# Second boundary turned from the residual itself, its root applied in the V, U and Z panels; first attention with four banks for head 0's logits

## The reference

```python
# first block
logits = q @ k * 64**-0.5 + bias         # banded attention, 16 heads, 128-token blocks, window +-128
x = x + rmsnorm(mixed, post_mix)
h = rmsnorm(x, pre_mlp)
f = square(relu(h @ w_mlp_in)) @ w_mlp_out
x = x + rmsnorm(f, post_mlp)             # residual 2
# second block, layer A
u, v, z = split(rms_norm(x, a_pre) @ a_w_in, 3)     # 3 x 2048 columns
v = layer_norm(gelu(v))
y = gelu(u) * (w_s v + b_s) * silu(z)
# rms_norm(x, g) = x * rsqrt(mean(x*x) + eps) * g, the root is one number per token
```

## Time and profile before

| | |
|---|---|
| median of 3 runs | 1885.99 us (1885.85 to 1886.63) |
| the profiled execution | 1886.83 us, its span 1885.0 us |
| PE busy (matmul) | 1819.4 us (97%) |
| PE weight load busy | 1511.0 us (80%) |
| DVE, ACT, POOL busy | 900.7, 855.2, 843.0 us (48%, 45%, 45%) |
| mean granted TensorE clock | 0.986 |
| chain that ended last | PE 80%, DVE 8%, issue 6%, ACT 3%, POOL 1% |

### The profile page before, as it was taken

How to read it: one execution, slowest core, us unless ns; L and a number is a source line. 1 busy time by engine, 2 the same in 40 slices (tenths; PEclk the granted TensorE clock), 3 DMA queues, 4 the chain that set the end, 5 groups by cost and what they waited for, 6 DMA issues and landing times.

```text
span 1885.0 us, 27143 instructions
## 1 busy us (share of the span) xinstructions
PE 1819.4 (97%) x9064; PEld 1511.0 (80%) x9064; DVE 900.7 (48%) x1331; ACT 855.2 (45%) x1795; POOL 843.0 (45%) x601
## 2 busy tenths in 40 slices
PE   8999999999899999999999999989999999999998
PEld 7787887888787788887988888867888888887776
DVE  4787898888414565234331033050063311446754
ACT  4655545555334656334442244243533332456662
POOL 4644555556453121444444444444364444432322
PEclk9999999999899999999999999989999999999999
DMA  5822121111133131332233333324232223221111
GB/s 173 145 79 68 56 67 56 59 64 57 45 101 118 35 106 39 97 131 91 89 90 101 99 92 100 99 71 155 78 109 81 90 85 100 84 70 57 58 44 56
DMA packets 46223, 159.85 MB, mean 85 GB/s; under 512 B 4763, under 2 KB 7195, under 8 KB 45884
## 3 DMA queue, kind: packets, MB, share of 16 engines
q1 hardware_dynamic: 38592, 140.53, 24.0%
q10 hardware_dynamic: 7548, 18.20, 3.9%
HBM read 152.42 MB, written 6.29 MB: 84 GB/s over the span
## 4 chain that ended last, share of the span: by engine, by line
PE 80%; DVE 8%; issue 6%; ACT 3%; POOL 1%; DVEq 0%; ACTq 0%; POOLq 0%
PE main L300 61%; PE main L328 4%; PE aux L772 3%; PE main L1702 2%; PE aux L759 1%; DVE u_acc L1904 1%; PE aux L746 1%; PE aux L372 1%; PE aux L603 1%; DVE x_res L547 1%; PE aux L627 1%; PE aux L747 1%; PE aux L636 1%; PE aux L1790 1%; DVE small L796 1%
## 5 line engine op out<-in xcount | busy, mean ns | idle before, releaser
L263 POOL TENSOR_TENSOR w_lo<-raw,w_hi 128x512 fp32r<-128x512 f32 x504 | 700.8, 1397 | 926.4 <-ACT w_hi L259 911.7
L259 ACT ACTIVATE w_hi<-raw 128x512 fp32r<-128x512 f32 x486 | 305.1, 631 | 702.9 <-PE main L300 689.2
L300 PE MATMUL main<-w_hi,a_hi 128*128 128x512 f32 x736 | 306.4, 416 | 1.7 <-ACT vv L1447 1.4
L300 PE MATMUL main<-w_hi,a_lo 128*128 128x512 f32 x736 | 289.8, 394 | 0.0
L300 PE MATMUL main<-w_lo,a_hi 128*128 128x512 f32 x736 | 289.1, 393 | 0.0
L300 PE MATMUL main<-a_hi,w_hi 128*128 128x512 f32 x576 | 230.4, 400 | 1.6 <-ACT u_raw L1199 1.6
L300 PE MATMUL main<-a_hi,w_lo 128*128 128x512 f32 x576 | 225.1, 391 | 0.0
L300 PE MATMUL main<-a_lo,w_hi 128*128 128x512 f32 x576 | 225.0, 391 | 0.0
L300 PEld LDWEIGHTS main<-w_hi,a_lo 128*128 128x128 f32 x736 | 139.3, 189 | 30.6
L300 PEld LDWEIGHTS main<-w_hi,a_hi 128*128 128x128 f32 x736 | 139.7, 190 | 28.3 <-issue 2.0
L300 PEld LDWEIGHTS main<-w_lo,a_hi 128*128 128x128 f32 x736 | 140.1, 190 | 23.3
(11 more groups left out here) (322 smaller groups left out, 3177.8 us busy)
## 6 DMA issues: line engine op xcount, KB each, us to landing
raw<-w_stream_in SPq DMA_DIRECT2D x264, 512.0 KB, 3.6
x_res<-x_in ACTq DMA_DIRECT2D x8, 512.0 KB, 5.0
rel_rows<-rel_row ACTq DMA_DIRECT2D x1, 4096.0 KB, 44.3
bias<-rel_rows ACTq DMA_DIRECT2D x2, 1536.0 KB, 7.7
out<-x_res SPq DMA_DIRECT2D x4, 512.0 KB, 2.6
bgate<-b_gate_in ACTq DMA_DIRECT2D x4, 256.0 KB, 5.3
ln_g<-ln_g_in ACTq DMA_DIRECT2D x1, 1024.0 KB, 5.6
ln_b<-ln_b_in ACTq DMA_DIRECT2D x1, 1024.0 KB, 7.7
```

What stands on the lines that cost most here:

```text
L259: eng.activation(w_hi[:, k, :], raw[:, k, :], ACT.Copy).then_inc(hi_done, 1)
L263: eng.tensor_tensor(w_lo[:, k, :], raw[:, k, :], w_hi[:, k, :].bitcast(F32), ALU.subtract).then_inc(lo_done, 1)
L300: mm = eng.matmul(mb[m][:, :], lhs, rhs, start=(first and k == 0 and n == 0), stop=(last and k == KT - 1 and n == 2))
```

## The change

It has two independent parts.

**Second boundary.** x_res, without the norm's root, is what PE turns (op2 reads x_res, PE waits for residual.wait_new instead of norm_xn). New orders act_turn_late, dve_turn_late and pool_turn_late: DVE does take, sums, gain and add for blocks 0, 1, 2 without anything between, then a_lo 0 and 1, block 3, a_lo 3 and on; the squares of x_res (act_one) stand on ACT behind a_hi 5, 7, 10, 12; one mean over all four blocks on DVE behind the last a_lo, one root on POOL in front of w_lo of the second V panel. The four scalings are gone. ACT waits for the squares before its loads and for the root before the first Gelu, and the root is the scale operand of the sixteen Gelus of V, sixteen of U and sixteen Silus of Z.

**First attention.** The logits of head 0 go to ab[0..3], all four behind m = 1, and DVE adds the bias to all four behind q_lo 0, then q_lo 1, maximum, q_lo 2, q_lo 3. The second attention is as before.

```diff
@@ class RowNorm
+            def dve_mean(self, eng):
+                eng.wait_ge(norm_sq, self.i * NT + NT)
+                v = small[:, self.s:self.s + NT]
+                eng.tensor_scalar(v, v, 1.0 / DM, EPS, ALU.mult, ALU.add).then_inc(norm_ms, NT)
+            def pool_root(self, eng):
+                eng.wait_ge(norm_ms, self.i * NT + NT)
+                v = small[:, self.s:self.s + NT]
+                eng.tensor_tensor(v, v, minus_half.broadcast_to((P, NT)), ALU.pow).then_inc(norm_rs, NT)
...
@@ pe_logits
+                if t == 0 and self.w == 384:
+                    if c == 0:
+                        eng.wait_ge(biased, one_up(j * 32 + self.b * 32))
+                        eng.wait_ge(p_in, one_up(j * 32 + self.b * 32))
+                        eng.wait_ge(att_out, one_up(j * 8 + self.b * 8))
+                elif c >= 2 or t > 0:
...
+            def logit_bank(self, t, c):
+                return ab[c if t == 0 and self.w == 384 else c % 2]
@@ dve_query
                 self.dve_take_q(eng, j, [0])
+                if self.w == 384:
+                    self.dve_logits(eng, j, 0)
+                    self.dve_take_q(eng, j, [1])
+                    self.dve_max(eng, ch, j, 0)
+                    self.dve_take_q(eng, j, [2, 3])
+                    return
@@
-        norm2 = RowNorm(2, fb, junk, 12)
-        op2 = HalfOperand("op2", fb, [to_a(lambda k: col("a_pre", k))])
+        norm2 = RowNorm(2, None, junk, 12)
+        op2 = HalfOperand("op2", x_res, [to_a(lambda k: col("a_pre", k))])
...
+        def act_turn_late(act, res, norm, op, p, spare, og):
+            for k in range(NSP):
+                spare_hi(act, spare, p, k)
+            res.act_sq(act, 1, og, [0])
+            for k in range(NSP, KT):
+                spare_hi(act, spare, p, k)
+            res.act_sq(act, 1, og, [1])
+            res.act_sq(act, 1, og, [2])
+            for i in range(4):
+                op.act(act, i)
+            res.act_sq(act, 1, og, [3])
+            for i in range(4, 2 * KT):
+                op.act(act, i)
+                if i in (5, 7, 10, 12):
+                    norm.act_one(act, {5: 0, 7: 1, 10: 2, 12: 3}[i], lambda e, m: res.wait_new(e, m))
+                if i >= KT and i < KT + NSP:
+                    next_hi(act, p + 1, i - KT)
+        def dve_turn_late(dve, ch, res, norm, op, og, p):
+            def new(m):
+                res.dve_ms_one(dve, m)
+                res.dve_gain(dve, ch, 1, [m])
+                res.dve_add_one(dve, m)
+            for m in (0, 1, 2):
+                res.dve_take(dve, 1, add=True, og=og, p=p, ms=[m])
+                new(m)
+            for i in range(2):
+                op.dve(dve, i)
+            res.dve_take(dve, 1, add=True, og=og, p=p, ms=[3])
+            op.dve(dve, 2)
+            new(3)
+            for i in range(3, 2 * KT):
+                op.dve(dve, i)
+            norm.dve_mean(dve)
+        def pool_turn_late(pool, res, norm, p, spare):
+            for k in range(4):
+                spare_lo(pool, spare, p, k)
+            res.pool_one(pool, 0)
+            for k in range(4, NSP):
+                spare_lo(pool, spare, p, k)
+            res.pool_one(pool, 1)
+            res.pool_one(pool, 2)
+            spare_lo(pool, spare, p, 6)
+            res.pool_one(pool, 3)
+            spare_lo(pool, spare, p, 7)
+            norm.pool_root(pool)
...
@@ scalar
-            act_turn(act, res2, norm2, op2, P_MLP + 16, spare2, O_MLP + 11, add=True)
+            act_turn_late(act, res2, norm2, op2, P_MLP + 16, spare2, O_MLP + 11)
             act.wait_ge(op2.turned, 2 * KT)
+            act.wait_ge(norm_sq, 3 * NT)
...
             hi(P_V + 1, [6])
+            norm2.act_wait_root(act)
...
-                    act.activation(gu[:, m, :], mb[m][:, :], ACT.Gelu_apprx_tanh).then_inc(bank_free, 1)
+                    act.activation(gu[:, m, :], mb[m][:, :], ACT.Gelu_apprx_tanh, scale=norm2.root(m)).then_inc(bank_free, 1)
...
@@ tensor
-                for c in {1: (0, 1), 2: (2, 3)}.get(m, ()):
+                for c in ({1: (0, 1, 2, 3)} if att is att1 else {1: (0, 1), 2: (2, 3)}).get(m, ()):
...
-                            tail_panel(base + 7, ob + 5, fo, first=False, k_off=8, turn=(op2, norm2))
+                            tail_panel(base + 7, ob + 5, fo, first=False, k_off=8, turn=(op2, res2))
...
-            head_panel(op2, norm2, P_V, O_V, ao, False, spare2)
+            head_panel(op2, res2, P_V, O_V, ao, False, spare2)
```

More of the change, by code:

```diff
@@ L470, in pe_wait @@
             def pe_wait(self, eng, m):
-                eng.wait_ge(norm_xn, self.i * NT + m + 1)
+                eng.wait_ge(norm_xn, self.scaled * NT + m + 1)
         minus_half = small[:, 0:1]
@@ L527, in dve_gain, with dve_wait_gain @@
                     ch(eng.scalar_tensor_tensor(f, f, math.sqrt(DM), g_row[:, n * NCOL:(n + 1) * NCOL], ALU.mult, ALU.mult))
-            def dve_wait_gain(self, eng, m, add):
-                if not add:
-                    eng.wait_ge(bank_free, (self.og + 1) * 4 + m + 1)
+            def dve_wait_gain(self, eng, m):
+                eng.wait_ge(bank_free, (self.og + 1) * 4 + m + 1)
             def dve_ms_one(self, eng, m):
@@ L743, in pe_logits @@
                     eng.wait_ge(biased, one_up(j * 32 + self.b * 32))
+                bank = self.logit_bank(t, c)
                 lo, nb, off = self.span(c)
                 q, keys = self.q_hl[half][:, r, c * P:c * P + P], slice(lo * P, (lo + nb) * P)
-                eng.matmul(ab[c % 2][:, 0:nb * P], q, self.k_hh[half][:, keys], start=True, stop=False)
-                eng.matmul(ab[c % 2][:, 0:nb * P], q, self.k_ll[half][:, keys], start=False, stop=True).then_inc(logits, 1)
+                eng.matmul(bank[:, 0:nb * P], q, self.k_hh[half][:, keys], start=True, stop=False)
+                eng.matmul(bank[:, 0:nb * P], q, self.k_ll[half][:, keys], start=False, stop=True).then_inc(logits, 1)
+            def logit_bank(self, t, c):
+                return ab[c if t == 0 and self.w == 384 else c % 2]
             def turned_bank(self, t, c):
@@ L958, in dve_turn @@
                 gain(m)
-                res.dve_wait_gain(dve, m, add)
+                res.dve_wait_gain(dve, m)
                 res.dve_add_one(dve, m)
@@ L964, in dve_turn @@
             gain(2)
-            res.dve_wait_gain(dve, 2, add)
+            res.dve_wait_gain(dve, 2)
             res.dve_add_one(dve, 2)
@@ L1120, in _ @@
             pool.tensor_tensor(f, f, minus_half.broadcast_to((P, (G - NORMED) * NT)), ALU.pow).then_inc(y_rs, 1)
[L1121 to L1125, removed]
+            with pool.Fori(P_SSD + 1, P_MLP) as p:
+                for k in range(KT):
+                    make_lo(pool, p, k)
+            pool_turn(pool, res1, norm1, P_MLP, spare1)
+            with pool.Fori(P_MLP + 1, P_V) as p:
+                for k in range(KT):
+                    make_lo(pool, p, k)
+            pool_turn_late(pool, res2, norm2, P_V, spare2)
             with pool.Fori(P_V + 1, P_UZ + 1) as p:
@@ L1446, in _ @@
                     wait_full(act, P_V + n, O_V + n, m)
-                    act.activation(vv[:, m, n * NCOL:(n + 1) * NCOL], mb[m][:, :], ACT.Gelu_apprx_tanh,
+                    act.activation(vv[:, m, n * NCOL:(n + 1) * NCOL], mb[m][:, :], ACT.Gelu_apprx_tanh, scale=norm2.root(m),
                                    accum_out=small[:, 64 + n * 4 + m:65 + n * 4 + m]).then_inc(bank_free, 1)
@@ L1470, in take_z @@
                     act.wait_ge(yt_turned, one_up(j * 4))
-                    act.activation(sz2[:, m, :], mb[m][:, :], ACT.Silu).then_inc(bank_free, 1)
+                    act.activation(sz2[:, m, :], mb[m][:, :], ACT.Silu, scale=norm2.root(m)).then_inc(bank_free, 1)
             def gmlp_act(j):
@@ L2114, in _ @@
             res2.dve_gain(dve, ch, 0)
[L2115 removed]
+            dve_turn_late(dve, ch, res2, norm2, op2, O_MLP + 11, P_MLP + 15)
             dve.wait_ge(bank_free, 4 * (O_V + 4))
```

32 lines of the change are left out of this document (18 added, 14 removed).

## The result

| | median | executions | ratio to the kernel before, with its 95% interval |
|---|---|---|---|
| before | 1885.92 us | 1884.84 to 1886.63 (4) | |
| changed | 1873.71 us | 1871.65 to 1874.01 (4) | 0.9934 [0.9919, 0.995] |

A forecast was written before the change was run, and what follows sets the result against it. The kernel was taken as bound by PE nearly throughout. Second boundary 6.2 us plus first attention 3.2 us made 9.4 us: profiled 1877.4 us, median 1876.6 us, range 1873.5 to 1880.5.

The forecast's parts named there:

- I take POOL to be first: Second boundary, block 2: POOL's w_lo tile 6 goes ahead of DVE's add, which ends at 1249.5; head panel starts about 1249.95.
- Up to the add of block 0, nothing changes: Second boundary: DVE's work through the add of block 0 keeps its old times, ending at 1240.41.
- half step 3: Head panel behind the second boundary: this half step starts at 1255.85 instead of 1263.25, a gain of 7.4 us.
- The rival with DVE first: DVE starts both adds or the small operation ahead of POOL: 1.0 to 1.5 us better, 1875.3; chance 0.15.
- The clock at the boundary: New gap of about 1.6 us before the head panel may lower PE's clock: 0.3 us taken off, bounds 0 to 2.3.
- the slower rival: PE runs at 1.2 GHz through most of the head panel, using up the gain: 1886 to 1900; chance 0.02.
- later clock falls that come or go: Clock changes further back as all behind is moved: no term in the sum, the remaining chance of 0.05.
- The last wait in front of half step 3: Head panel: PE still waits about 1.0 us for a_lo 3, whose block's add runs behind POOL tile 7.
- The scale operand: V, U and Z evacuations: 0.096 us more each; costs 0.1 us behind the head panel, 0.8 at U and Z ends.
- ACT does not bound the head panel: Answers the rival that four squares of 1.2 us show in the head panel: 4.8 us, 1881.4; chance 0.09.
- Attention: First attention, both passes: waits for biased logits shrink and pass 1 keeps its clock; 3.35 us, 3.2 taken, ends 0 and 5.1.
- The forecast's first case: First attention: DVE's small operation beats POOL's four w_lo tiles, then ACT is late; PE's values start at 603.7 instead of 604.95.

The follow-up runs named there:

- e2: The changed kernel with the first attention put back as before, so the second boundary part alone; 1878.85 us, ratio 0.9954.
- e4: The changed kernel with the root left out as scale of the 48 evacuations of V, U and Z (output misses the root there); 1872.69 us, ratio 0.9933.
- e8: The changed kernel with sixteen extra 128x128 matmuls, results unused, behind the fourth V panel; 1877.86 us, ratio 0.9963.
- e10: The changed kernel run and profiled a second time, unchanged; 1872.20 us, ratio 0.9934.
- e3: The changed kernel with POOL's w_lo tile 7 in front of the root of block 3 instead of right behind it; 1873.61 us, ratio 0.9937.
- e5: The changed kernel with the load of the gain row issued one panel and a half earlier; 1872.90 us, ratio 0.9931.

## Why the prediction fell short

The direction and the mechanism held; the median came 2.9 us below the one forecast. The profiled time (1873.53 us) is 3.9 us below its forecast of 1877.4: 2.4 us from the second boundary, 1.7 from the gap behind the third, 0.4 from the attention, less 0.3 in the other stages and 0.3 outside the span.

**Block 2 of the boundary: the step that failed.** The forecast says "I take POOL to be first". It took the start of the add (1247.1) and the release of POOL's slot (1247.1) to be the same moment, which e2 shows to be right to 0.04 us, and then chose by what POOL had done in one trace. But in that trace DVE had already lost an earlier race, and the forecast carried its outcome over: four gains in 5.84 us. "Up to the add of block 0, nothing changes" is the sentence in which it slipped: by the shifted times the four gains end 1.3 us earlier (1230.57 + 3.48 against 1235.38), add 0 starts 0.6 us earlier, and add 2 0.6 us earlier than forecast (1243.00 + 3.48 against 1247.1) and takes 1.28 instead of 2.3 us. Together that is the 1.7 us at the start of the head panel. The step in the forecast's own terms: half step 3 gains 9.35 us (1263.25 - 1225.65 against 1250.42 - 1222.17) instead of 7.4. Where both races were lost (e2), it gains 7.7. The rival with DVE first had a price of 1.0 to 1.5 us and the chance 0.15; four of the seven profiles with this order of the code up to there showed it, at 1.65 us (0.6 for the first race, 1.05 for the second).

By the Trainium skill, page "SBUF — State Buffer", section "Who interferes with whom", the engine that starts first holds the shared port for its whole instruction. The traces agree: the add takes 1.28 us where it starts 0.56 us ahead of POOL and POOL's tile then takes 1.87 us, and 2.33 us where POOL starts 0.04 us ahead with 1.29.

**The clock at the boundary: forecast -0.3, measured 0.** No gap was left in the winning kind, and in the losing kind (e2, e4, e8) the clock stayed full as well behind 1.40 us. The head panel at 1.2 GHz, the slower rival, is not seen anywhere.

**The clock elsewhere: forecast 0 ("later clock falls that come or go"), measured 1.7 us.** It is the gap behind the third boundary, low in the profile before and full in the changed kernel's. This is no term of the change that a profile of before could give; its size could have been read there (PEclk 0.77 and 0.66 over 6 us), and the range, whose lower end held only the boundary's own better case with the full gain of the attention, had no room of its own for it. The part on the time before calls the clock full in 38 of 40 slices; but the digit 9 of the page stands for 90% or more, and three falls lie in such slices: this one, the one of pass 1, and one behind the first boundary (0.80 in the mean over 17 us). The last did not change in the first profile; in e10 it was half as long, and 1.6 us came of it.

**What held.** The last wait in front of half step 3: 0.59 us, forecast 1.0. The scale operand: 689 against 600 ns, and 1.0 us over V to Z against 0.9 forecast; e4 takes it to zero. The squares and POOL's root of 128x4 (1266.41, 1.02 us) make PE wait for nothing; ACT does not bound the head panel. Attention: 3.6 us against 3.2. The forecast's first case came, by a somewhat other way: POOL's four tiles started at 597.12 and the small operation at 596.62, 0.5 us apart, because ACT's copies came later than before; the first logits of head 1 were biased from 600.16 (forecast 600.25), PE's values began at 603.75 (forecast 603.7) behind ACT.

## What to carry to other kernels

When two engines that share a port are due within some tenths of a microsecond, the profile shows one outcome of a race, not its duration: look for the load or the engine whose spread decides it, price both outcomes, and ask whether the same spread feeds a second race behind. Account for a result by stages at fixed points of the program and not by the sum alone; where executions of one kernel lie 2 to 4 us apart, a second profile of the same kernel tells which stage belongs to the change. Ordering the rival's instruction in front of a wait, as e3 does, removes such a race at no cost that its stages show.

## What was not expected of the hardware

- The operation that waits for the gain row's load starts 3.37 to 3.73 us behind its issue, by the execution; through two races, these 0.1 to 0.4 us go with 1.65 us at the head panel.
- The engines share the loss: where DVE is first by 0.56 us, POOL's 1.28 us become 1.87.
- Behind a gap of 2.27 us the granted clock is low for a while in 4 of 12 profiles and full in 8, at a price of 1.6 us; at the first boundary it falls in all twelve and costs 1.7 us (e10, mean 0.90 over 17 us) or 3.4 us (before and changed, 0.80).
- Early arrival of DVE's operand is worth nothing where PE's own k step is the limit (e5: DVE 1 us, PE 0).
